# Projection, gated-recurrence scan and attention of a two-layer hybrid step: projection groups issued between the units of the scan, two a unit in units 1 to 7

## The reference

```
h = x * (1 + sc1) + sh1
cols = h @ w_in                     # 1024 -> 672 (MLA) + 1280 (HG) + 1152 (RW)
q = rmsnorm(q_c) @ w_uq ; kv = rmsnorm(ckv) @ w_ukv
mla_o = softmax(q k^T) v            # 8 heads, cached keys for the sample
hg_o, s = hgrn_scan(q, i, zf_fwd, zf_bwd) * silu(g)   # both directions, 4 heads
rw_o, s = rwkv_scan(token_shift(rw_cols), ...)
mix = concat(mla_o, hg_o, rw_o) @ w_out
x = layernorm(ALPHA * x + g1 * mix)
x = layernorm(ALPHA * x + g2 * expert_choice(x * (1 + sc2) + sh2))
```

## Time and profile before

| what | us |
|---|---|
| median of 3 runs (lowest, highest) | 3207.37 (3201.31, 3212.47) |
| span of the profiled execution | 3198.3 |
| project, layer 0 and layer 1 | 220.6 and 220.2 |
| attention, layer 0 and layer 1 | 203.5 and 202.5 |
| hgrn scan, layer 0 and layer 1 | 175.7 and 175.5 |

### The profile page before, as it was taken

One profiled execution on the slowest core, in us unless ns is written; L12 is line 12 of the kernel. 1 busy time (PEld: TensorE's weight loads), 2 busy tenths in 40 slices (PEclk: granted clock), 3 DMA queues, 4 the chain that ended last, 5 costly groups with the idle time before them and its releaser, 6 DMA issues. The chain is left out here.

```text
span 3198.3 us, 72152 instructions
## 1 busy us (share of the span) xinstructions
PE 2651.5 (83%) x32434; PEld 1804.7 (56%) x32434; DVE 1152.6 (36%) x2476; ACT 464.6 (15%) x957; POOL 754.8 (24%) x886
## 2 busy tenths in 40 slices
PE   6997865688784899999889978556886859999995
PEld 3564545538633666766545645455485356667672
DVE  1003668774534111111130046786745241111112
ACT  1003340042111000000020033302311010000001
POOL 0003818334213000000010055372441220000002
PEclk8999996889886999999999999878998969999997
DMA  7101000050053899999831010001400459999994
GB/s 275 53 0 39 1 10 3 1 218 4 28 203 128 323 393 396 399 392 399 307 125 40 0 39 1 10 3 60 160 30 9 204 185 379 398 391 395 396 372 140
DMA packets 73209, 552.68 MB, mean 173 GB/s; under 512 B 13848, under 2 KB 15704, under 8 KB 33992
## 3 DMA queue, kind: packets, MB, share of 16 engines
q1 hardware_dynamic: 66760, 527.11, 41.5%
q0 software_dynamic: 6144, 20.98, 2.9%
HBM read 523.54 MB, written 24.51 MB: 171 GB/s over the span
## 5 line engine op out<-in xcount | busy, mean ns | idle before, releaser
L2359 PEld LDWEIGHTS ps<-arena 128*64 128x64 f32 x16384 | 577.8, 138 | 90.0 <-issue 87.4
L2359 PE MATMUL ps<-arena 128*64 128x80 f32 x16384 | 598.4, 234 | 14.2 <-issue 9.6
L2373 PE MATMUL ps<-arena 128*80 128x512 f32 x1024 | 466.8, 600 | 0.0
L2434 DVE TENSOR_TENSOR arena<-arena,ps 128x160 f32<-128x160 f32 x128 | 41.1, 321 | 720.4 <-ACT arena L2394 720.4
L524 PE MATMUL ps<-arena 128*128 128x128 f32 (+1 forms) x1088 | 294.7, 434 | 4.5 <-DVE arena L577 4.5
L2373 PEld LDWEIGHTS ps<-arena 128*80 128x80 f32 x1024 | 143.9, 150 | 229.6 <-issue 218.7
L524 PEld LDWEIGHTS ps<-arena 128*128 128x128 f32 x1088 | 164.4, 191 | 134.9 <-issue 130.0
L2394 ACT ACTIVATE arena<-ps 128x160 f32<-128x160 f32 x128 | 38.8, 303 | 1006.9 <-PE ps L2359 1006.9
L2120 POOL DMA_INDIRECT sum_d<-arena x32 | 45.6, 1426 | 583.5 <-DVE arena L2426 583.5
L581 DVE COPY arena<-ps 128x128 f32<-128x128 f32 (+3 forms) x48 | 16.3, 341 | 397.7 <-PE ps L524 285.9
L2114 POOL DMA_INDIRECT arena<-h_d,arena x32 | 40.2, 1256 | 497.9 <-DVEq L2409 430.4
(11 more groups left out here) (343 smaller groups left out, 3901.1 us busy)
## 6 DMA issues: line engine op xcount, KB each, us to landing
arena<-in_ex_w SPq DMA_DIRECT2D x128, 2048.0 KB, 15.7
arena<-in_ex_w SPq DMA_DIRECT2D x128, 1024.0 KB, 13.9
arena<-in_ada_w SPq DMA_DIRECT2D x32, 1024.0 KB, 7.8
arena<-in_w_t SPq DMA_DIRECT2D x34, 512.0 KB, 3.3
arena<-in_ada_w SPq DMA_DIRECT2D x8, 2048.0 KB, 16.0
arena<-in_w_tok SPq DMA_DIRECT2D x2, 3712.0 KB, 17.3
h_d<-x_sb SPq DMA_DIRECT2D x10, 512.0 KB, 2.6
sum_d<-x_sb SPq DMA_DIRECT2D x10, 512.0 KB, 13.5
```

Source lines behind the costliest of these rows:

```text
L2359: m = nc.tensor.matmul(gated(j)[c * 64:(c + 1) * 64, f, a, :], w13[q % WG][:, a, k, f * P + c * 64:f * P + (c + 1) * 64], xT[:, x % 2, k, ...
L2373: m = nc.tensor.matmul(rows_out(x, h), he[:, x % 2, f, :], w2[:, q % WP, f % 2, h * 512:(h + 1) * 512], start=f == 0, stop=f == KD - 1)
L2434: nc.vector.tensor_tensor(he[:, b, 2 * j:2 * j + 2, :], hs[:, j % 2], gated(j)[:, :, 1, :], ALU.mult).then_inc(S["he"], 1)
```

## The change

project and hgrn become one phase, **phase_mix**, ahead of the attention; the attention is then followed by rwkv directly. PE first makes q and z for the prompt tile, the values of tile 0, and q and z for the other tiles. The other 32 large groups are tied two by two into 16 items: five of MLA columns (m), two of the gate (g), nine of RWKV (r). Item 0 comes ahead of unit 1; units 1 to 7 hold two items each, one after the scores and one at the unit's end; units 8 and 9 hold none; item 15 stands after the last normalising product. Items use two PSUM banks in turn, scores three banks in turn in place of five, outputs and states their three as before. ACT empties all items, and applies the silu of q and g and DVE the clip of z while they empty a bank.

To make room, weights lie where results come later, or in x_sb: the first six chunks in the memory of rwT and gT, the rest in x_sb (a ring of five chunks for r). x is therefore written to a buffer x_d in device memory at the end of layer 0 and loaded again (2560 KB) at the start of each attention, behind that phase's weights; output waits for it. The query levels keep one buffer for each direction, so the levels of a unit wait for the scores of the unit before it in the same direction. The token shift uses the memory of hgT.

The core of the diff:

```diff
-WRING = 6
+WRING = 5
...
-    def q_level(u, j, a):
-
-        if u % 4 != 3:
-            return QL[u % 2][:, j, a]
-        if j < TILES:
-            return tok[:, j, (2 + a) * P:(3 + a) * P]
-        return tok[:, 2 * (j - TILES) + a, 4 * P:5 * P]
...
+    groups = [("x", t, h) for t in range(TILES) for h in range(2)]
+    NX = len(groups)
+    groups += [("q", c, 0) for c in range(2)] + [("z", c, 0) for c in range(4)] + [("v", 0, 0)]
+    groups += [("q", c, 1) for c in range(2)] + [("z", c, 1) for c in range(4)]
+    NH = len(groups)
+    groups += [("v", t, 0) for t in range(1, TILES)]
+    NV = len(groups)
+    groups += [("m", t, s) for t in range(TILES) for s in range(2)]
+    NM = len(groups)
+    groups += [("g", c, s) for c in range(2) for s in (1, 0)]
+    NGT = len(groups)
+    groups += [("r", c, s) for c in range(NRW) for s in (1, 0)]
+    N = len(groups)
...
-        if u >= 4:
-            eng.wait_ge(S["at_ps"], NG * (u - 3))
+        if u >= 2:
+            eng.wait_ge(S["at_ps"], NG * (u - 1))
...
+            if l:
+                sp.wait_ge(S["st_xd"], 16 * TILES * l)
+            sp.wait_ge(S["pj_ps"], NX)
+            sp.dma_start(w_m1, d["w_m1"][l]).then_inc(S["ld_m1"], 16)
+            sp.dma_start(w_m2a, d["w_m2"][l, :, 0:6]).then_inc(S["ld_m2"], 16)
...
+            sp.wait_ge(S["pj_ps"], NM)
+            for c in range(NRW):
+                if c >= WRING:
+                    sp.wait_ge(S["pj_ps"], NGT + 2 * (c - WRING + 1))
+                sp.dma_start(e.x[:, c % WRING, :].rearrange("p (k n) -> p k n", k=KD), d["w_t"][l, HGT + 2 + c]
...
+            for n in range(NH):
+                project(n)
+            scores(0)
+            turn(0)
+            evacuated(pe, NX + 6)
+            project(NH)
+            project(NH + 1)
+            chunk_state(0)
+            project(NH + 2)
+            project(NH + 3)
+            for m in range(NH, NV):
+                evacuated(pe, m)
+            item(0)
+            for u in range(1, U):
+                scores(u)
+                if units[u] not in last:
+                    turn(u)
+                if u < 8:
+                    item(2 * u - 1)
+                out(u - 1)
+                if units[u] not in last:
+                    chunk_state(u)
+                if u < 8:
+                    item(2 * u)
+            out(U - 1)
+            pe.wait_ge(S["hg_sq"], 2)
+            for p in range(2):
+                nc.tensor.matmul(ps[:, 2 + 2 * p, :], e.blk[:, :], sq[:, p, 0:512], start=True, stop=True)
+                nc.tensor.matmul(ps[:, 3 + 2 * p, 0:P], e.blk[:, :], sq[:, p, 512:NTOK], start=True, stop=True
+                                 ).then_inc(S["hg_ss"], 1)
+            item(15)
...
+            for n in range(0, NX, 2):
+                evacuate(n)
+            evacuate(NX)
+            evacuate(NX + 1)
+            sigmoids(0)
+            evacuate(NX + 6)
+            evacuate(NX + 7)
+            evacuate(NX + 8)
+            sigmoids(1)
+            turned(0)
+            for n in range(NH, NV):
+                evacuate(n)
+            item(0)
+            for u in range(1, U):
+                if units[u] not in last:
+                    turned(u)
+                if u < 8:
+                    item(2 * u - 1)
+                    item(2 * u)
...
+            for c in range(4):
+                clip(NX + 2 + c)
+                dve.wait_ge(S["pj_dve"], NX // 2 + c + 1)
+                dve.sem_inc(S["hg_z"], 1)
             prepare(0)
             for _ in run_levels(0):
                 pass
-            prepare(1)
+            for c in range(4):
+                clip(NX + 9 + c)
+                dve.wait_ge(S["pj_dve"], NX // 2 + 4 + c + 1)
...
+                if u == 0:
+                    prepare(1)
...
+            evacuated(dve, NGT - 1)
...
+            dve.wait_ge(S["pj_ps"], N)
...
+            sp.dma_start(e.x[:, :, :], (e.x_d if l else d["x"]).rearrange("(t p) n -> p t n", p=P)).then_inc(S["ld_xr"], 16)
...
+                if more:
+                    sp.dma_start(e.x_d[t * P:(t + 1) * P, :], x[:, t, :]).then_inc(S["st_xd"], 16)
...
-    (phase_modulation, MODULATION_SEMS), (phase_project, PROJECT_SEMS), (phase_attention, ATTENTION_SEMS),
-    (phase_hgrn, HGRN_SEMS), (phase_rwkv, RWKV_SEMS), (phase_output, OUTPUT_SEMS), (phase_route, ROUTE_SEMS),
+    (phase_modulation, MODULATION_SEMS), (phase_mix, MIX_SEMS), (phase_attention, ATTENTION_SEMS),
+    (phase_rwkv, RWKV_SEMS), (phase_output, OUTPUT_SEMS), (phase_route, ROUTE_SEMS),
```

More of the change, by code:

```diff
@@ new lines, in phase_mix, with evacuated, pbank @@
+    groups += [("m", t, s) for t in range(TILES) for s in range(2)]
[4 more added lines that the diff above has]
+    N = len(groups)
+    by_act = [n % 2 == 0 if g[0] == "x" else g[0] != "z" for n, g in enumerate(groups)]
+    def evacuated(eng, n):
+        own = by_act[n]
+        eng.wait_ge(S["pj_act" if own else "pj_dve"], sum(a == own for a in by_act[:n + 1]))
+    def pbank(n):
+        return n % 8 if n < NX else n % 2
@@ L498, in _ @@
         def _(sp):
[L499 to L506 removed]
+            for c in range(HGT):
+                sp.dma_start(hw[c], d["w_t"][l, c]).then_inc(S[f"ld_hw{c}"], 16)
@@ L509, in _, with project @@
         def _(pe):
[L510 to L515, removed]
+            def project(n):
+                kind, a, s = groups[n]
+                if n < NX:
+                    if n >= 8:
+                        evacuated(pe, n - 8)
+                elif n == NX:
+                    for m in range(NX - 2, NX):
+                        evacuated(pe, m)
+                elif n > NX + 1:
+                    evacuated(pe, n - 2)
+                dst = ps[:, pbank(n), :]
@@ L549, in _ @@
+            out(U - 1)
[5 more added lines that the diff above has]
+            item(15)
         @block.scalar
         def _(act):
-            for n in range(0, len(groups), 2):
+            a = e.chain("act", act)
@@ new lines, in _ @@
+            act.wait_ge(S["hg_o"], 1)
+            for src, n in SEG:
+                nc.scalar.activation(sq[:, :, n], src, ACT.Square).then_inc(S["hg_sq"], 1)
+            for p in range(2):
+                act.wait_ge(S["hg_ss"], p + 1)
+                nc.scalar.activation(rs[:, p, :], ps[:, 2 + 2 * p:4 + 2 * p, :].rearrange("p a b -> p (a b)")[:, 0:NTOK], ACT.Sqrt,
+                                     bias=e.eps[:, 0:1], scale=1.0 / HD).then_inc(S["hg_rt"], 1)
+            item(15)
+            e.done("act", a)
@@ new lines, in _ @@
+        @block.gpsimd
+        def _(pool):
+            c = e.chain("pool", pool)
+            nc.gpsimd.memset(qz, 0.0).then_inc(S["hg_zero"], 1)
+            nc.gpsimd.memset(KL[0], 0.0).then_inc(S["hg_kl0"], 1)
+            c.add(nc.gpsimd.memset(KL[1], 0.0))
+            c.join()
+            k = 0
+            for u, (t, dr) in enumerate(units):
+                if dr == 0:
+                    continue
+                if k < 2:
+                    pool.wait_ge(S["hg_prep"], k + 1)
+                    pool.wait_ge(S["hg_q"], 2 * k + 2)
+                for _ in levels(nc.gpsimd, c, u):
+                    pass
+                k += 1
+                pool.sem_inc(S["lv1"], 1)
+            pool.wait_ge(S["pj_ps"], NGT)
+            for col in (0, pad_at(NPR) - 1, PAD - 1):
+                nc.gpsimd.memset(e.rwT[:, :, col:col + 1], 0.0).then_inc(S["rw_pad"], 1)
+            e.done("pool", c)
```

764 lines of the change are left out of this document (374 added, 390 removed).

## The result

Runs of both kernels taken in turn: before 3204.8 us (median, 3201.3 to 3212.5), after 3014.2 us (3012.8 to 3018.9). The ratio is 0.941, 95% interval 0.9392 to 0.9428: 190 us faster. The forecast was 3037 us (3015 to 3085). The median lies 0.8 us under the low end of that range; the ratio, applied to the 3207.4 us that the forecast started from, gives 3018. The profiled execution of after took 3014.45 us by its own clock, with a span of 3012.2 us, so 2.2 us lie around the span. The 9.1 us that the prediction carried was the distance between one execution's span and the median of others.

What follows compares the result with a forecast made beforehand. TensorE limits project but in the scan waits for VectorE. Merging saves 86.4 and 85.8 us, together 172, less 2 in the attention: span 3198.3 to 3028.3; with the median's 9.1 us carried, 3037 us (3015 to 3085).

Steps and rivals of the forecast that it cites:

- The merged stage: Project and scan as one stage, laid out on TensorE: 309.9 us a layer in place of 396.3 and 395.7.
- the scan's own products: Scores, state transpose, output and chunk state on TensorE with a warm clock: 7.8 us a unit, 78 for ten.
- the 4 us of stalls and handoffs: Merged stage, emptying: 0.6 us for a last copy, 0.3 for handoffs in each of seven units, 1.3 for last masks.
- Cost 0: Merged stage: TensorE never waits for forward or backward levels; smallest margin 5 us, in units 8 and 9.
- rival B: Merged stage: the clock stays low; at 0.67 the time is 3269 us, slower; break-even at 0.73; chance 0.06.
- The end: From the last output to the merged stage's end: 16.6 us, of which 8.7 already counted in the projection, so 7.9.
- its own work is the same: Attention: no longer stands behind the scan, and its work is unchanged; only slower weight loads would lengthen it.
- The term itself (reload of x): Attention: reload issued behind the weights, taken as 1 us a layer, with 0 and 6.5 as the ends.
- A: Merged stage: the scan's waits stay visible in units 1 to 7, 44 us a layer, 3125 us; chance 0.12.
- D: Merged stage: no overlap, items and scan strictly serial with the old prologue, near 3207 us; chance 0.02.
- C: Attention: reload of x delays the weights 6.5 us a layer, 3048 us; sign: longer weight wait; chance 0.08.
- The carry to the median: Whole kernel: the runs' median stands 9.1 us above the profiled span, and this difference is added to the forecast.

Runs made afterwards that it cites:

- the load experiment: Changed kernel with 40 more VectorE fills in the second half of each forward level set of units 2, 4, 6 and 8: 3075.5 us, ratio 0.9598.
- the last kernel above: Changed kernel with only the clearing of semaphores moved behind the first loads, in the attention and in rwkv: 3010.6 us, ratio 0.9393.

## Why the prediction was right, and where it was off

**What bounds.** Right: with the scan's products put beside the items, TensorE is the limit throughout, busy 295.3 of 302.4 us.

**The merged stage.** 309.9 forecast, 302.4 measured. By pieces, forecast and measured: start 10.1 and 9.3; head 55.5 and 55.4; scores(0) to scores(1) 31.2 and 28.7; units 1 to 7 179.7 and 174.7; units 8 and 9 16.9 and 17.6; end 16.6 and 16.7. The mis-sized terms are the scan's own products, 78, and the 4 us of stalls and handoffs: the 0.3 us a handoff did not exist, a unit's own work is 7.55 us with a state product and 6.65 in units 1 and 2 without one, where I took 7.8 for all; and of the first and last units' parts 1.8 us fell away. The saving was so 14.5 us larger than 172 (of it 1.4 since the stages before were 395.9 and 397.5 us by block ends, not 396.3 and 395.7).

**Levels.** "Cost 0" was right, and the interleaving is why: taken apart, it costs 41 us of waits in layer 0. But the working behind it, VectorE's work against the length of two units, was the wrong measure; the load experiment missed by 58 us for it. The right one is each half's deadline, 10.5 us away.

**The clock.** Right at 0.99 and 0.98; rival B is out. The items themselves keep TensorE busy, and the same small products run at 1.00 between items and at 0.87 on average where waits return. The Trainium skill (TensorE: Matmul & The Clock Gate, A second HAM failure mode: psum-queue depth-cycling) tells of a clock that oscillates where TensorE goes round PSUM banks and idles briefly between groups. Here scores went round three banks and items two, but the brief idles were missing (174.70 of 174.7 us busy), so its condition was not met there; where waits are back, at 0.87, no run tells the going round of banks from the idle time.

**The end.** 16.6 forecast, 16.7 measured, and by the route forecast: counted from the end of the last output, item 15 starts at 6.0 us (6.0) and ends at 14.8 (14.7), the reciprocals end at 13.4 (13.2), and VectorE's last products wait for item 15. The block products ran at half clock behind a gap of 2 us, as they had before.

**Attention.** Forecast +1 us a layer, measured +4.9 and +2.6. The step that failed is "its own work is the same": the merged stage has 47 semaphores and the old projection 10, and SyncE clears them ahead of the loads. The term itself (reload of x) was 0. The 1.3 us that the prediction took from the earlier trace rows as the wait of TensorE's first product is a sum over both of TensorE's queues, products and weight loads; of the products' own waits in the kernel before only layer 1 has one for this load:

```profile
PE ps L684 <- DMA arena<-in_c_kr: 0.4, 1, 0.4
```

So the wait grew from nothing and 0.4 us to 3.0 in each layer. Why some 1.2 us a layer more remain isn't settled. What the merged stage leaves behind is not shown to be the reason: the transposes that follow the wait start at 0.64 us a pair in layer 0, but at 0.38 (the second pair; 0.44 the first) in the last kernel above, whose merged stage ends the same way and whose wait is 0.9 us. In layer 0 another 3.2 us is product time further on: from 362.5 to 551.7 us the last 1354 products are busy 166.4 us at clock 0.97, where before the same number took 163.2 at 0.99; in layer 1 they take 163.2 again.

**Rivals.** A and D: no wait for state, masks or levels. C: its sign appeared, since the wait for the attention's weights grew to 3.0 us, but not its cause: with the reload issued later the wait stays (2.7 and 3.4 us), with the clearing issued later it falls to 1.1 us and to none. Only put ahead of the weights does the reload cost its 6.3 us.

**The carry to the median.** 9.1 us in place of 2.2: 7 us of the 23 by which 3037 was high. 14.5 more came from the stage and 7 from rwkv, which the forecast had left alone, less 5.5 in the attention: 23. The 7 us of the carry are luck of the execution that was profiled, rwkv's may be in part, and the misses of stage and attention partly cancel.

## What to carry to other kernels

Work laid between the steps of a dependent chain must be checked by the deadline of each piece (when its input comes, when its consumer stands in the queue), not by an engine's sum over a period; but once no consumer waits, where the items stand no longer matters (two orders here, 3014.2 and 3013.3 us). In this kernel an idle us on TensorE cost 1.3 to 1.4 us where small products lie around it (54.0 us lost for 41.1 of waits, 14.1 for 10.6, 26.1 for 18.3). When phases are merged, look at what the next phase's start inherits: here 47 semaphores to clear ahead of its first load.

## What the runs showed of the hardware

Clearing 47 semaphores on SyncE takes 2.8 us, about 0.06 us each: ahead of the first load they put it 2.7 and 3.1 us after the block's start in the two layers, behind the loads it leaves after 0.1 us or less. One SyncE DMA issue now and then takes 2.0 to 2.2 us in place of 0.5 (one of the attention's loads in layer 0, in two of the profiles). A fill of 128x256 on VectorE takes 0.27 us; in a row of 40, each waiting for the one before, they start 0.39 us apart.
